# High and low parts for three chunks of the keys and for the merge's first branch, in a two-block transformer kernel

## The chip, the cores and the metric

The kernel runs on one core of a Trainium2 chip. The number compared is the device time of one execution in microseconds (us). The kernel before takes 986.09 us, the median of three runs (984.8 to 986.31). A row of the profile gives a start in us from the start of the span.

TensorE (PE in the rows) multiplies matrices into PSUM, the accumulation memory of eight banks. ScalarE (ACT), VectorE (DVE) and GpSimd (POOL) do elementwise work, and SyncE (SP) issues the transfers of the weights. Each engine works through its own queue in order; semaphores order them among each other.

## The reference, cut to what matters

256 tokens of width 1024 go through two blocks. The change lies in the first 240 us, in the first block's mixer and in the key and value projection of its cross-attention:

```python
proj = h @ w_in                                    # 1024 -> 6144
a = a_val * sigmoid(a_gate)
a = causal_dwconv(a, conv_a_w) + conv_a_b          # 31 taps, 512 channels
a = silu(layernorm(a, ln_a_g, ln_a_b)) @ w_a_out   # 512 -> 1024
p = grouped(multiscale_pool_minus_token(u_pool)) * pool_scale
c = (c_b * causal_dwconv(c_c * c_x, conv_c_w)) @ w_c_out
merged = gates[0] * a + gates[1] * p + gates[2] * c
x = x + merged @ w_o
k, v = split(mem_n @ w_xkv, 2)                     # 256 memory rows, 1024 -> 2048
```

## The kernel before, in words

**Chunks and halves.** All large weights come as one stream of chunks, each of two halves of 128 partitions by 1024 numbers (512 KB). SP loads half `c` into one of six raw buffers (`raw`, RAW = 6), as soon as half `c - 6` has left it. `C_WIN`, `C_K1`, `C_V1`, `C_POOL`, `C_MERGE`, `C_V1B`, `C_WO` are the first chunks of the input projection (24 chunks), the keys (4), three of four value chunks (3), the pool (1), the merge (4), the last value chunk (1) and the output projection (4). I write K0 to K3 for the chunks of the keys, V0 to V2 for those of the values, M0 to M3 for the merge, and "first half" and "second half" for the halves of each.

**Two ways to multiply.** A half whose number is in `NATIVE` is multiplied as it is, in float32, straight from `raw` (`project_native`), and its raw buffer comes free when TensorE has used it. Any other half is split: ScalarE rounds it to `wh` (`round_high`, L1685 in the rows), VectorE subtracts to get `wl` (`subtract`, L2183), which frees the raw buffer, and TensorE multiplies three products, high by high, high by low and low by high (`three`). There are four slots of `wh` and `wl` (SPLIT = 4), so ScalarE may round a half only when TensorE has used the split half four before it. `after(n)` lets an engine go ahead in this splitting up to two chunks behind chunk `n`; `full(n)` does so up to the next chunk and then waits until TensorE is done with chunk `n`.

**Units.** The result of a chunk (or of half a merge chunk) is a unit, and goes to one of four PSUM banks (UNITS = 4) in turn. `free_bank` makes TensorE wait until the unit four before it has been read, by ScalarE or by VectorE.

**Order around the change.** TensorE: input projection, K0 to K3 with `memn` (the normalised memory rows), V0, the sum for the layer norm's mean, V1, the sum for its variance, V2, four small pool units, then for each m of the merge the product of branch a (native, with `actT`, the output of the silu) and of branch c (split, with `cy_h` and `cy_l`), V1B, and the output projection. VectorE does the 124 instructions of the 31 taps in portions between the splits (`convolve`, L2303), then the layer norm's elementwise part, the pool's four units (L2416), and for each m the merge's products with the gates, their sum and its split for the next projection. The order on each engine is written out by hand; no scheduler changes it.

Of the kernel before, what the change touches and what calls it, by code (L numbers as in the profile page):

```python
# [28 lines left out]
ALU = mybir.AluOpType  # L29
# [7 lines left out]
P = 128  # L37
# [44 lines left out]
CHUNKS = C_FFN + 3 * FSTEPS  # L82
HALVES = 2 * CHUNKS

NATIVE = frozenset((*range(4), *range(2 * C_K1, 2 * C_K1 + 8), 2 * C_POOL, 2 * C_POOL + 1, *range(2 * C_MERGE, 2 * (C_MERGE + 4), 2),
                    *range(2 * C_K2, 2 * C_K2 + 2), *range(2 * C_FILL, 2 * C_FILL + 8), 2 * C_V2B, 2 * C_V2B + 1,
                    *range(2 * C_FFN, 2 * C_FFN + 4)))

# [117 lines left out]
def build(nc, stream, xt_in, memt_in, mem2t_in, small_in, const_in, mask_in, router_in, moe_in, gain_in, out_rows):  # L206
    ctx = ExitStack()
    with ctx:
        def sb(name, shape, dt=F32):
            return ctx.enter_context(nc.sbuf_tensor(name, shape, dt))  # L210

        def sem(name):
            return ctx.enter_context(nc.semaphore(name))
# [7 lines left out]
        xT = sb("xT", [P, DK, T])  # L221
        sq_at = -(-nc.sbuf_base // 32) * 32
        sq = sb("sq", [P, DK, T])
        memn = sb("memn", [P, 2, DK, T])
        kT = sb("kT", [P, DK, T])
        vm = sb("vm", [P, TT, D])
# [33 lines left out]
        def at(name, start, shape, dt):  # L260
            return nc.alloc_sbuf_tensor_at(name, shape, dt, offset=area_at + 4 * start)
# [55 lines left out]
        cpad_at = r.at  # L317
        cpad = r(4, T + C_K - 1)
        cy_h, cy_l = (at(n, start, [P, 4, T], F32R) for n, start in (("cy_h", cpad_at), ("cy_l", cx_at)))
        upad = r(4, T + PADW)  # L320
        ubuf = r(4, T + PADW)

# [2 lines left out]
                                 for i in range(4))  # L325
        asq = agate
        actT = memn[:, 0, 0:4, :]

        xg32 = kT
        vm_flat = vm.rearrange("p t d -> p (t d)")  # L330
# [162 lines left out]
        ln_std = sem("ln_std")  # L493
        ln_normed = sem("ln_normed")
        a_act = sem("a_act")
        pool_full = sem("pool_full")
        merged_ready = sem("merged_ready")
        scores_done = sem("scores_done")
# [213 lines left out]
        def _(pe):  # L712
            units = UnitCount()

            def matmul(out, w, x, start, stop, **kw):
                return nc.tensor.matmul(out, w, x, start=start, stop=stop, **kw)  # L716

            def wait_raw(c):

                pe.wait_ge(landed[c % RAW], 16 * (c // RAW + 1))  # L720

            def wait_split(c):
                pe.wait_ge(low_ready, split_count(c))

            def free_bank(u):

                if u >= UNITS:
                    before = u - UNITS
                    pe.wait_ge(act_free if before in ACT_UNITS else unit_free, act_count(before) if before in ACT_UNITS else freed(before + 1))

            def three(out, a_h, a_l, b_h, b_l, start, stop, **kw):

                matmul(out, a_h, b_h, start, False, **kw)
                matmul(out, a_h, b_l, False, False, **kw)
                return matmul(out, a_l, b_h, False, stop, **kw)
# [276 lines left out]
            def project_native(n, x, tile_ready=None, between=None):  # L1012

                u = units.take()
                free_bank(u)
                for j in range(2):
                    c = 2 * n + j
                    if c:
                        wait_raw(c)
                    else:  # L1020
                        pe.wait_ge(s_first, 16)
                    for k in range(DK):
                        if c == 0 and k == DK // 2:
                            wait_raw(c)
                        if tile_ready and j == 0:
                            pe.wait_ge(tile_ready, k + 1)
                        last = matmul(psum[:, u % UNITS, j * T:(j + 1) * T], raw[:, c % RAW, k * P:(k + 1) * P],
                                      x[:, k, :], k == 0, k == DK - 1)
                    last.then_inc(half_done, 1)
                    if between and j == 0:  # L1030
                        between()
# [28 lines left out]
            for n in range(C_WIN + 16, C_WIN + 24):  # L1060
                project(n, xg)
            pe.wait_ge(memn_ready, 1)
            for m in range(4):
                project_native(C_K1 + m, memn[:, 0])
                if m == 2:
                    stats(2)

            pe.wait_ge(mem_split, 1)
            project_rows(C_V1, xg)
            pe.wait_ge(ln_added, 1)  # L1070
            for c in range(2):
# [12 lines left out]
            for m in range(4):  # L1084
# [6 lines left out]
                        last.then_inc(half_done, 1)  # L1091
                if m < 3:
                    last.then_inc(pool_full, 1)
            pe.wait_ge(a_act, 4)
            pe.wait_ge(c_split, 1)
            for m in range(4):
                c = 2 * (C_MERGE + m)
                wait_raw(c)
                u = units.take()
                free_bank(u)  # L1100
                for j in range(2):
                    for k in range(4):
                        last = matmul(psum[:, u % UNITS, j * T:(j + 1) * T],
                                      raw[:, c % RAW, k * 256 + j * P:k * 256 + (j + 1) * P], actT[:, k, :],
                                      k == 0, k == 3)
                last.then_inc(half_done, 1)
                wait_split(c + 1)
                u = units.take()
                free_bank(u)
                for j in range(2):  # L1110
                    for k in range(4):
                        w = slice(k * 256 + j * P, k * 256 + (j + 1) * P)
                        last = three(psum[:, u % UNITS, j * T:(j + 1) * T], wh[:, SLOT[c + 1], w], wl[:, SLOT[c + 1], w],
                                     cy_h[:, k, :], cy_l[:, k, :], k == 0, k == 3)
                last.then_inc(half_done, 1)
            project_rows(C_V1B, xg)
            pe.wait_ge(merged_ready, 4)
            for m in range(4):
# [491 lines left out]
        def _(act):  # L1610
# [145 lines left out]
            from_unit(C_V1 + 1, 29, vm[:, :, 256:512])  # L1756
            act.wait_ge(ln_var, 1)
            fn(lnstd, psum[:, 5, 0:T], ACT.Sqrt, scale=1.0 / 512, bias=eps[:]).then_inc(ln_std, 1)
            act.wait_ge(ln_normed, 2)
            for c in range(4):  # L1760
                fn(actT[:, c, :], aacc[:, c, :], ACT.Silu, scale=sm("ln_g", c), bias=sm("ln_b", c)).then_inc(a_act, 1)
            from_unit(C_V1 + 2, 30, vm[:, :, 512:768])

            def divide(hh):

# [404 lines left out]
        def _(dve):  # L2170
# [167 lines left out]
            def short_conv(j):  # L2338
# [7 lines left out]
                                                      ALU.mult, ALU.add)  # L2346
                link(last)

            for n in range(4, 24):
                if n in (8, 9):  # L2350
                    full(C_WIN + n)
                    h = slice(2 * (n - 8), 2 * (n - 8) + 2)
                    dve.wait_ge(act_free, act_count(7))
                    tt(cpad[:, h, C_K - 1:], unit_view(n), cx[:, h, :], ALU.mult).then_inc(unit_free, 1)
                after(C_WIN + n)
                convolve(5 if n < 6 else 4)
                if n == 6:
                    window_sums()
                if n == 7:
                    window_means()  # L2360
                if n == 10:
                    dve.wait_ge(unit_free, freed(10))
                if 10 <= n < 13:
                    short_conv(n - 10)
                if n == 13:
                    dve.wait_ge(act_free, act_count(11))
                    tt(cy[:], cy[:], cb[:], ALU.mult).then_inc(c_ready, 1)
                if n == 17:
                    recip(1)
                if n == 20:  # L2370
                    normalise_memory(0, "mem_g")
# [10 lines left out]
            split_memory(0, xh, xl)  # L2382
            for n in range(4):
                after(C_K1 + n)
                convolve(10 if n < 3 else 4 * CONV_K - done[0])
            dve.wait_ge(conv_a, 4 * CONV_K)
            tt(asq[:, 0:2, :], aacc[:, 0:2, :], aacc[:, 2:4, :], ALU.add).then_inc(ln_added, 1)
            recip(2)
# [15 lines left out]
            for m in range(2):  # L2404
                h = slice(2 * m, 2 * m + 2)
                tt(aacc[:, h, :], aacc[:, h, :], two(lnrstd), ALU.mult).then_inc(ln_normed, 1)
            after(C_V1 + 2)
            dve.wait_ge(act_free, act_count(23))
            for m in range(4):
                if m < 3:  # L2410
# [8 lines left out]
                last.then_inc(unit_free, 1)  # L2419
            for m in range(4):  # L2420
                full(C_MERGE + m)
                ua, uc = units.take(), units.take()
                q = slice(2 * m, 2 * m + 2)
                tt(mt1[:], unit_view(ua), gates[:, 2 * m:2 * m + 2, :], ALU.mult).then_inc(unit_free, 1)
                tt(mt2[:], unit_view(uc), gates[:, 16 + 2 * m:18 + 2 * m, :], ALU.mult).then_inc(unit_free, 1)
                dve.wait_ge(unit_free, freed(uc + 1))
                link(tt(mt1[:], mt1[:], mt2[:], ALU.add))
                link(tt(merged[:, q, :], mt1[:], merged[:, q, :], ALU.add))
                link(v.tensor_copy(yh[:, q, :], merged[:, q, :]))
                tt(yl[:, q, :], merged[:, q, :], f32(yh[:, q, :]), ALU.subtract).then_inc(merged_ready, 1)  # L2430
                after(C_MERGE + m)
# [689 lines left out]
def _stream(a):  # L3121
# [14 lines left out]
    units(C_WIN, a["w_in"][0], WIN_ORDER)  # L3136
    s[C_POOL, 1] = a["w_pool_grp"][0].transpose(1, 0, 2).reshape(P, 1024)
    for m in range(4):
        s[C_MERGE + m, 0] = _tiles(a["w_a_out"][0], 4, 256 * m, 256)
        s[C_MERGE + m, 1] = _tiles(a["w_c_out"][0], 4, 256 * m, 256)  # L3140
    units(C_K1, a["w_xkv"][0], range(4))
    units(C_V1, a["w_xkv"][0], range(3), D, row_halves)
    units(C_V1B, a["w_xkv"][0], (3,), D, row_halves)
# [106 lines left out]
```

## Time and profile before

| | us |
|---|---|
| median of three runs | 986.09 |
| the profiled execution's own time | 987.19 |
| its span, from the first to the last instruction | 985.3 |
| PE busy with matmuls | 964.8 (98%) |
| DVE busy | 750.9 (76%) |
| ACT busy | 518.7 (53%) |
| POOL busy | 40.5 (4%) |

All figures but the first are of one profiled execution, which took 1.1 us more than the median of the runs; 1.9 us of its time lie outside the span. A PE row's duration is the time of one matmul from its issue to its end; several are on their way at a time, so the pace is read from the starts, or from the number of matmuls in a stretch. A native float32 product shows as two records.

### The profile page before, as it was taken

The page shows a single profiled execution, that of the slowest core. Times are in us where ns is not written, and L with a number is a line of the kernel's source. Part 1 is how long each engine was busy: PE and PEld are TensorE (multiplying, and loading weights), DVE is VectorE, ACT ScalarE, POOL GpSimd, SP SyncE. Part 2 cuts the span into 40 slices and gives each one's busy share as a digit, 9 for nine tenths or more (in the row PEclk, how much of TensorE's full clock was granted, in tenths as well). Part 3 has the DMA queues.
Part 4 walks back from the last instruction along what each step waited for, and adds up shares of the span by engine and source line. Part 5 has one row for each costly group of instructions (what it writes and reads, how often), then busy time and mean ns, then how long its engine had stood idle before and what let it go on. Part 6 is the DMA issues. An engine that isn't in the chain of part 4 may idle for free.

```text
span 985.3 us, 16653 instructions
## 1 busy us (share of the span) xinstructions
PE 964.8 (98%) x6545; PEld 886.5 (90%) x6545; DVE 750.9 (76%) x1137; ACT 518.7 (53%) x752; POOL 40.5 (4%) x42
## 2 busy tenths in 40 slices
PE   7999999999999999999999999999999999999997
PEld 6999998999999888888889999877999998999996
DVE  5699878779766886888868877965486289787876
ACT  4545533524453676777754635545465465555544
POOL 0002001000101000000001000000100120000000
PEclk9999999999999999999999999999999999999999
DMA  7945653456540677878873534221543255555541
GB/s 273 354 161 177 211 166 128 171 172 218 171 143 1 235 259 274 322 264 292 319 255 122 174 95 168 65 66 65 192 170 131 86 191 192 192 179 200 178 168 43
DMA packets 49601, 178.39 MB, mean 181 GB/s; under 512 B 5632, under 2 KB 5888, under 8 KB 49280
## 3 DMA queue, kind: packets, MB, share of 16 engines
q1 hardware_dynamic: 47952, 172.51, 51.3%
q10 hardware_dynamic: 1584, 4.99, 1.4%
q8 instruction: 44, 0.72, 0.3%
q14 instruction: 21, 0.17, 0.1%
HBM read 176.43 MB, written 1.05 MB: 180 GB/s over the span
## 4 chain that ended last, share of the span: by engine, by line
PE 91%; DVE 6%; issue 1%; DMA 1%; ACT 1%; DVEq 0%; SPq 0%; ACTq 0%
PE psum L716 89%; DVE wl L2183 2%; DVE work L2183 1%; DMA raw<-stream_in 1%; DVE xl L2221 1%; PE psum L958 1%; PE psum L1270 0%; DVE work L3012 0%; DVE xh L2216 0%; DVE rstd L2211 0%; DVE xT L2183 0%; ACT wh L1685 0%; DVE work L3075 0%; DVE ypair L2183 0%; ACT work L1612 0%
## 5 line engine op out<-in xcount | busy, mean ns | idle before, releaser
L1685 ACT CAST wh<-raw 128x1024 fp32r<-128x1024 f32 x292 | 303.8, 1051 | 288.4 <-PE psum L716 248.5
L2183 DVE TENSOR_TENSOR wl<-raw,wh 128x1024 fp32r<-128x1024 f32 x292 | 349.3, 1228 | 72.4 <-ACT wh L1685 69.5
L716 PE MATMUL psum<-xh,wh 128*128 128x256 f32 x976 | 275.9, 283 | 2.9 <-DVE wl L2183 2.3
L716 PE MATMUL psum<-xl,wh 128*128 128x256 f32 x976 | 273.1, 280 | 0.0
L716 PE MATMUL psum<-xh,wl 128*128 128x256 f32 x976 | 273.1, 280 | 0.0
L716 PEld LDWEIGHTS psum<-xh,wh 128*128 128x128 f32 x976 | 184.2, 189 | 6.3 <-DVE wl L2183 2.6
L716 PEld LDWEIGHTS psum<-xl,wh 128*128 128x128 f32 x976 | 184.2, 189 | 0.5
L716 PEld LDWEIGHTS psum<-xh,wl 128*128 128x128 f32 x976 | 184.2, 189 | 0.0
L716 PE MATMUL psum<-wh,slots 128*128 128x512 f32 x320 | 101.6, 390 | 0.0
L716 PE MATMUL psum<-memn,raw 128*128 128x256 f32 x320 | 73.0, 381 | 0.0
L716 PE MATMUL psum<-yh,wh 128*128 128x256 f32 x256 | 72.1, 282 | 0.2 <-DVE wl L2183 0.2
L716 PE MATMUL psum<-yh,wl 128*128 128x256 f32 x256 | 71.6, 280 | 0.0
L716 PE MATMUL psum<-yl,wh 128*128 128x256 f32 x256 | 71.4, 279 | 0.0
L716 PEld LDWEIGHTS psum<-wh,slots 128*128 128x128 f32 x320 | 60.1, 188 | 12.4
L716 PEld LDWEIGHTS psum<-memn,raw 128*128 128x128 f32 x320 | 59.4, 190 | 8.1 <-issue 0.7
L716 PE MATMUL psum<-wl,slots 128*128 128x512 f32 x160 | 62.3, 389 | 0.0
L2183 DVE TENSOR_TENSOR work<-psum,rstd 128x512 f32<-128x512 f32 x38 | 26.0, 690 | 41.1 <-PE psum L716 40.9
L2303 DVE SCALAR_TENSOR_TENSOR ypair<-work,small,ypair 128x256 f32<-128x256 f32 x120 | 54.8, 523 | 0.0
L2138 POOL TENSOR_TENSOR sq<-sq 128x512 f32<-128x512 f32 x18 | 27.0, 1501 | 551.2 <-ACT sq L1612 550.9
L716 PEld LDWEIGHTS psum<-yh,wh 128*128 128x128 f32 x256 | 48.1, 188 | 1.1 <-issue 0.7
L716 PEld LDWEIGHTS psum<-yl,wh 128*128 128x128 f32 x256 | 48.1, 188 | 0.0
L716 PEld LDWEIGHTS psum<-yh,wl 128*128 128x128 f32 x256 | 48.1, 188 | 0.0
(277 smaller groups left out, 1478.8 us busy)
## 6 DMA issues: line engine op xcount, KB each, us to landing
raw<-stream_in SPq DMA_DIRECT2D x325, 512.0 KB, 4.5
memn<-mem_t_in ACTq DMA_DIRECT2D x2, 1024.0 KB, 9.1
out_rows<-work SPq DMA_DIRECT2D x4, 256.0 KB, 2.2
const<-const_in ACTq DMA_DIRECT2D x1, 581.0 KB, 4.7
xT<-x_t_in SPq DMA_DIRECT2D x2, 256.0 KB, 4.6
xT<-x_t_in ACTq DMA_DIRECT2D x2, 256.0 KB, 5.4
raw<-stream_in SPq DMA_DIRECT2D x2, 256.0 KB, 5.3
mask<-mask_in ACTq DMA_DIRECT2D x1, 512.0 KB, 13.6
```

The costliest lines, as they stand in the source:

```text
L716: return nc.tensor.matmul(out, w, x, start=start, stop=stop, **kw)
L958: last = nc.tensor.transpose(psum[:, u % UNITS, m * T + t * P:m * T + (t + 1) * P], probs[:, (base + h) % 4, t, m * P:(m + 1) * P], ident)
L1685: nc.scalar.copy(wh[:, SLOT[c], :], raw[:, c % RAW, :]).then_inc(hi_ready, 1)
L2138: nc.gpsimd.tensor_tensor(sq[:, 0:2, :], sq[:, 0:2, :], sq[:, 2 * m:2 * m + 2, :], ALU.add).then_inc(sq_added, 1)
L2183: return v.tensor_tensor(out, a, b, op)
L2221: last = v.scalar_tensor_tensor(xl[:, k, :], xT[:, k, :], sm(name, k), f32(xh[:, k, :]), ALU.mult, ALU.subtract)
L2303: ins = v.scalar_tensor_tensor(aacc[:, c, :], x, sm("conv_w", 4 * j + c), aacc[:, c, :], ALU.mult, ALU.add)
```

## The change

1. K1 to K3 leave `NATIVE` and are split; K0 stays native. TensorE waits for the split of the memory rows (`mem_split`) after K0 and not after K3.
2. The merge: branch a is split as well. Its activations get a high part `ay_h`, made by ScalarE, and a low part `ay_l`, made by VectorE. For each m branch c now comes first and branch a second, and the waits stand ahead of the first use of each.
3. ScalarE copies the values' third unit, with the splits that stand ahead of this copy, before the norm's activation, and not after it.
4. The 124 taps are spread anew over the chunks: 96 (before: 82) by the end of the input projection, then 5, 8, 8, 7 (before: 10, 10, 10, 12).

```diff
-NATIVE = frozenset((*range(4), *range(2 * C_K1, 2 * C_K1 + 8), 2 * C_POOL, 2 * C_POOL + 1, *range(2 * C_MERGE, 2 * (C_MERGE + 4), 2),
+NATIVE = frozenset((*range(4), 2 * C_K1, 2 * C_K1 + 1, 2 * C_POOL, 2 * C_POOL + 1,
...
             pe.wait_ge(memn_ready, 1)
-            for m in range(4):
-                project_native(C_K1 + m, memn[:, 0])
+            project_native(C_K1, memn[:, 0])
+            pe.wait_ge(mem_split, 1)
+            for m in range(1, 4):
+                project(C_K1 + m, xg)
                 if m == 2:
                     stats(2)
-            pe.wait_ge(mem_split, 1)
...
-            pe.wait_ge(a_act, 4)
-            pe.wait_ge(c_split, 1)
             for m in range(4):
...
+                for i, (high, low, ready) in enumerate(((cy_h, cy_l, c_split), (ay_h, ay_l, a_split))):
+                    c = 2 * (C_MERGE + m) + i
+                    wait_split(c)
+                    pe.wait_ge(ready, 1)
+                    u = units.take()
+                    free_bank(u)
+                    for j in range(2):
+                        for k in range(4):
+                            w = slice(k * 256 + j * P, k * 256 + (j + 1) * P)
+                            last = three(psum[:, u % UNITS, j * T:(j + 1) * T], wh[:, SLOT[c], w], wl[:, SLOT[c], w],
+                                         high[:, k, :], low[:, k, :], k == 0, k == 3)
+                    last.then_inc(half_done, 1)
...
             fn(lnstd, psum[:, 5, 0:T], ACT.Sqrt, scale=1.0 / 512, bias=eps[:]).then_inc(ln_std, 1)
+            from_unit(C_V1 + 2, 30, vm[:, :, 512:768])
             act.wait_ge(ln_normed, 2)
             for c in range(4):
                 fn(actT[:, c, :], aacc[:, c, :], ACT.Silu, scale=sm("ln_g", c), bias=sm("ln_b", c)).then_inc(a_act, 1)
-            from_unit(C_V1 + 2, 30, vm[:, :, 512:768])
+            act.wait_ge(a_act, 4)
+            nc.scalar.copy(ay_h[:], actT).then_inc(a_high, 1)
...
+            TAPS = {4: 5, 5: 5, 13: 4, 14: 6, 15: 6, 16: 6, 17: 4, 18: 6, 19: 6, 20: 3, 21: 5, 22: 6, 23: 6}
...
-                convolve(5 if n < 6 else 4)
+                convolve(TAPS.get(n, 4))
...
-                convolve(10 if n < 3 else 4 * CONV_K - done[0])
+                convolve((5, 8, 8)[n] if n < 3 else 4 * CONV_K - done[0])
...
             after(C_V1 + 2)
+            dve.wait_ge(a_high, 1)
+            tt(ay_l[:], actT, f32(ay_h[:]), ALU.subtract).then_inc(a_split, 1)
             dve.wait_ge(act_free, act_count(23))
...
-                ua, uc = units.take(), units.take()
+                uc, ua = units.take(), units.take()
                 q = slice(2 * m, 2 * m + 2)
+                tt(mt2[:], unit_view(uc), gates[:, 16 + 2 * m:18 + 2 * m, :], ALU.mult).then_inc(unit_free, 1)
                 tt(mt1[:], unit_view(ua), gates[:, 2 * m:2 * m + 2, :], ALU.mult).then_inc(unit_free, 1)
-                tt(mt2[:], unit_view(uc), gates[:, 16 + 2 * m:18 + 2 * m, :], ALU.mult).then_inc(unit_free, 1)
-                dve.wait_ge(unit_free, freed(uc + 1))
+                dve.wait_ge(unit_free, freed(ua + 1))
```

The two halves of each merge chunk change places in the stream, so that the weights of branch c come first.

ScalarE around the layer norm's activation, before (`work<-psum,eps` is the square root of the variance, `memn<-ypair,small` the silu, `vm<-psum` the copy of V2's unit, the casts split weights):

```order
L1612 ACTIVATE work<-psum,eps 128x256 [waits ln_var]
L1612 ACT_TABLE_LOAD
L1612 ACTIVATE memn<-ypair,small 128x256 [waits ln_normed]
L1612 ACTIVATE memn<-ypair,small 128x256 x3
L1685 CAST wh<-raw 128x1024 [waits half_done,landed5]
L1612 ACTIVATE vm<-psum 128x2x256 [waits half_done]
L1685 CAST wh<-raw 128x1024 [waits half_done,landed1]
```

The same place on ScalarE after the change:

```order
L1611 ACTIVATE work<-psum,eps 128x256 [waits ln_var]
L1684 CAST wh<-raw 128x1024 [waits half_done,landed4]
L1684 CAST wh<-raw 128x1024 [waits half_done,landed5]
L1611 ACTIVATE vm<-psum 128x2x256 [waits half_done]
L1611 ACT_TABLE_LOAD
L1611 ACTIVATE memn<-ypair,small 128x256 [waits ln_normed]
L1611 ACTIVATE memn<-ypair,small 128x256 x3
L1763 CAST ay_h_68<-memn 128x1024 [waits a_act]
```

The copy that waits for TensorE's V2 now stands ahead of the table load, of the silu and of the new cast.

VectorE from the end of the norm to the first merge unit, before (`work<-psum,small,work` reads a pool unit, two instructions each; `memn<-psum,work` is a merge product with its gate):

```order
L2183 TENSOR_TENSOR wl<-raw,wh 128x1024 [waits hi_ready]
L2416 SCALAR_TENSOR_TENSOR work<-psum,small,work 128x256 [waits pool_full,act_free]
L2416 SCALAR_TENSOR_TENSOR work<-psum,small,work 128x256
...
L2183 TENSOR_TENSOR wl<-raw,wh 128x1024 [waits hi_ready]
L2183 TENSOR_TENSOR memn<-psum,work 128x512 [waits half_done]
```

And after:

```order
L2184 TENSOR_TENSOR wl<-raw,wh 128x1024 [waits hi_ready] x2
L2184 TENSOR_TENSOR ay_l<-memn,ay_h 128x1024 [waits a_high]
L2420 SCALAR_TENSOR_TENSOR work<-psum,small,work 128x256 [waits pool_full,act_free]
L2420 SCALAR_TENSOR_TENSOR work<-psum,small,work 128x256
...
L2184 TENSOR_TENSOR wl<-raw,wh 128x1024 [waits hi_ready] x2
L2184 TENSOR_TENSOR memn<-psum,work 128x512 [waits half_done]
```

The reading of the pool's units now stands behind the subtraction that waits for ScalarE's `ay_h`, and where one half was split two are split.

## Rows read from the trace of the kernel before

**Rows 1.** The page, busy time of each engine

```profile
PE 964.8 (98%) x6545; PEld 886.5 (90%) x6545; DVE 750.9 (76%) x1137; ACT 518.7 (53%) x752; POOL 40.5 (4%) x42
```

**Rows 2.** Waits of PE over the span: total us, times, longest

```profile
PE psum L716 <- DMA raw<-stream_in: 5.8, 1, 5.8
PE psum L716 <- DVE wl L2183: 2.5, 4, 1.3
```

**Rows 3.** Windows: length, busy us of each engine, then granted clock, DMA share, GB/s

```profile
100.00:145.00 45.00, 45.00 (x386) 44.95 (x386) 39.33 (x65) 21.75 (x25) 0.00 (x0) 1.00 0.61 195
147.96:175.83 27.87, 27.87 (x132) 24.54 (x131) 23.84 (x41) 10.62 (x16) 4.75 (x4) 1.00 0.41 132
189.10:194.80 5.70, 5.70 (x50) 5.69 (x49) 3.04 (x3) 3.62 (x6) 0.00 (x0) 1.00 0.00 0
198.24:223.40 25.16, 25.16 (x161) 23.50 (x161) 19.03 (x29) 5.24 (x5) 0.00 (x0) 1.00 0.55 186
```

**Rows 4.** Timeline of ScalarE: start, length, instruction, count

```profile
178.51 1.04 ACT L1751 CAST cy_h<-work 128x1024 fp32r<-128x1024 f32 x1
...
189.31 0.47 ACT L1612 ACTIVATE work<-psum,eps 128x256 f32<-128x256 f32 x1 [0.27 <-PE psum L716]
189.80 1.28 ACT L1612 ACT_TABLE_LOAD   x1
192.93 2.08 ACT L1612 ACTIVATE memn<-ypair,small 128x256 f32<-128x256 f32 x4 [1.85 <-DVE ypair L2183]
...
195.85 0.59 ACT L1612 ACTIVATE vm<-psum 128x512 f32<-128x512 f32 x1
```

**Rows 5.** Timeline of VectorE, keys to pool

```profile
151.72 11.51 DVE L2303 SCALAR_TENSOR_TENSOR ypair<-work,small,ypair 128x256 f32<-128x256 f32 x20
...
174.65 4.83 DVE L2303 SCALAR_TENSOR_TENSOR ypair<-work,small,ypair 128x256 f32<-128x256 f32 x12
179.51 0.69 DVE L2183 TENSOR_TENSOR ypair<-ypair 128x512 f32<-128x512 f32 x1
...
197.13 3.22 DVE L2416 SCALAR_TENSOR_TENSOR work<-psum,small,work 128x256 f32<-128x256 f32 x8
```

**Rows 6.** Timeline of VectorE, merge and output projection

```profile
204.74 1.29 DVE L2183 TENSOR_TENSOR memn<-psum,work 128x512 f32<-128x512 f32 x2 [3.26 <-PE psum L716]
...
208.59 1.22 DVE L2183 TENSOR_TENSOR wl<-raw,wh 128x1024 fp32r<-128x1024 f32 x1
211.03 1.29 DVE L2183 TENSOR_TENSOR memn<-psum,work 128x512 f32<-128x512 f32 x2 [1.23 <-PE psum L716]
...
223.62 1.29 DVE L2183 TENSOR_TENSOR memn<-psum,work 128x512 f32<-128x512 f32 x2
...
227.46 2.35 DVE L2183 TENSOR_TENSOR wl<-raw,wh 128x1024 fp32r<-128x1024 f32 x2
...
233.25 2.35 DVE L2183 TENSOR_TENSOR wl<-raw,wh 128x1024 fp32r<-128x1024 f32 x2
...
237.70 2.35 DVE L2183 TENSOR_TENSOR wl<-raw,wh 128x1024 fp32r<-128x1024 f32 x2
240.50 0.69 DVE L2183 TENSOR_TENSOR xT<-psum,xT 128x512 f32<-128x512 f32 x1 [0.45 <-PE psum L716]
```

**Rows 7.** Timeline of GpSimd, keys

```profile
152.02 4.12 POOL L2138 TENSOR_TENSOR sq<-sq 128x512 f32<-128x512 f32 x3 [63.42 <-ACT sq L1612]
156.22 0.79 POOL L2142 TENSOR_TENSOR sq<-sq 128x256 f32<-128x256 f32 x1
```

**Rows 8.** Timeline of PE around 570 us

```profile
568.17 2.37 PE L716 MATMUL psum<-cden,const 10*64 10x256 f32 x20
...
572.20 0.41 PE L716 MATMUL psum<-xh,wl 128*128 128x256 f32 x1
572.41 0.41 PE L716 MATMUL psum<-xh,wh 128*128 128x256 f32 x1
```

**Rows 9.** Window on the same place, columns as in the third group

```profile
571.00:575.00 4.00, 4.00 (x23) 4.00 (x23) 3.12 (x8) 0.00 (x0) 0.00 (x0) 0.57 0.83 250
```

More of the change, by code:

```diff
@@ L223, in build @@
         sq = sb("sq", [P, DK, T])
+        memn_at = -(-nc.sbuf_base // 32) * 32
         memn = sb("memn", [P, 2, DK, T])
@@ L319, in build @@
         cy_h, cy_l = (at(n, start, [P, 4, T], F32R) for n, start in (("cy_h", cpad_at), ("cy_l", cx_at)))
+        ah_at = 24 * T + 8
+        assert ah_at + 4 * T <= 24 * T + 4 * (T + CONV_K - 1)
+        ay_h = at("ay_h", ah_at, [P, 4, T], F32R)
         upad = r(4, T + PADW)
@@ L327, in build @@
         actT = memn[:, 0, 0:4, :]
+        ay_l = nc.alloc_sbuf_tensor_at("ay_l", [P, 4, T], F32R, offset=memn_at)
         xg32 = kT
@@ L495, in build @@
         a_act = sem("a_act")
+        a_high = sem("a_high")
+        a_split = sem("a_split")
         pool_full = sem("pool_full")
@@ L1093, in _ @@
                     last.then_inc(pool_full, 1)
-            pe.wait_ge(a_act, 4)
-            pe.wait_ge(c_split, 1)
             for m in range(4):
[L1097 to L1115, printed above, removed]
+                for i, (high, low, ready) in enumerate(((cy_h, cy_l, c_split), (ay_h, ay_l, a_split))):
[10 more added lines that the diff above has]
+                    last.then_inc(half_done, 1)
             project_rows(C_V1B, xg)
@@ L3138, in _stream @@
     for m in range(4):
-        s[C_MERGE + m, 0] = _tiles(a["w_a_out"][0], 4, 256 * m, 256)
-        s[C_MERGE + m, 1] = _tiles(a["w_c_out"][0], 4, 256 * m, 256)
+        s[C_MERGE + m, 0] = _tiles(a["w_c_out"][0], 4, 256 * m, 256)
+        s[C_MERGE + m, 1] = _tiles(a["w_a_out"][0], 4, 256 * m, 256)
     units(C_K1, a["w_xkv"][0], range(4))
```

## The prediction

> **What bounds the kernel now.** I read first the page's busy times: PE is at work for 964.8 of the span's 985.3 us, VectorE for 76% [rows 1]. Then the waits of PE: 5.8 us for the first transfer and 2.5 us for splits in the whole span [rows 2]. So a microsecond less of matmul work shortens the kernel by as much, if the other engines keep up. Then windows, for the pace of each way to multiply. Three products: 386 matmuls in 45.00 us, 0.1166 each, so a half of 24 takes 2.80 us. Native: K0 to K3 are 64 products in 27.87 us, less 0.43 for one sum's product, so a half of eight takes 3.43 us [rows 3]. The merge, four native and four split units, takes 25.16 us, so a split unit there is 2.85 and a native one 3.44. Last the timelines of ScalarE and VectorE from 150 to 240 us, for who comes late once PE is faster.
>
> **Part 1, keys.** Six halves save 0.63 each: PE comes to V0 3.8 us sooner, at 172.0 and not 175.83. Does VectorE follow? It gains six subtractions, 1.15 us each where they stand in pairs [rows 6], and loses 14 of 42 taps, 0.40 each (12 in 4.83) [rows 5], to the input projection. There VectorE is busy for 39.33 of 45 us [rows 3], and its 14 taps are 5.6 us over that stretch of waits, which I cost at nothing; the price if that cover is gone is 0.40 a tap. ScalarE gains six casts of 1.04 and is busy for 10.62 of these 27.87 us [rows 3, 4]; they hide in its waits for PE. SP's loads wait for the last use of a raw buffer; that was PE's end of a native half and is now VectorE's subtraction, which comes sooner for all but K0, so I cost the transfers at nothing (0.39 to 0.61 of the transfer engines' time there is used [rows 3], and a late one would cost its delay in full). The last links before the norm's mean: the second half of V1 can be rounded only when PE ends K3 (172.0), one cast (1.04, the shape of the 178.51 row) [rows 4] makes that 173.2, its subtraction 174.35, seven taps 177.1, the sum of 0.69 [rows 5] 177.8. PE has V0 done at 172.0 + 5.7 = 177.7 [rows 3]. So 0.1 us of stall, and about half a microsecond of slack in the taps ahead of it. From there PE goes through two sums of 0.86 and V1 and V2 of 5.70 each: it ends V2 at about 190.95, where before it was 194.8 [rows 3]: 3.85 us ahead.
>
> **Part 2, ScalarE's copy ahead of the activation.** This is where I see the gain go. Before, the square root ran at 189.31, the table load right behind it at 189.80 while nothing else was due, the silu at 192.93, and the copy at 195.85 [rows 4]. Now the copy waits for V2 (190.95, seen at 191.15), and what stands behind it in the queue comes after it, although the norm is ready at about 189.1. Step by step: copy to 191.65 (the next instruction may follow 0.50 later), load 1.28, silu 2.08, so 195.05; `ay_h`, a cast of the same size as `cy_h`, 1.04, so 196.15; `ay_l` on VectorE, 1.22 with 1.15 to the next instruction, so 197.35 [rows 4, 6]. Behind it on VectorE wait the eight instructions that read the pool's units, 3.22 us for eight [rows 5], which took no input from the norm. The first bank comes free after two, at 198.2. PE is done with the pool at 190.95 + 3.44 = 194.4, and its first merge product needs that bank. Before, the reading began at 197.13 [rows 5] and PE started the merge at 198.24 [rows 3]. Now it starts at 198.3. All 3.85 us of part 1 have turned into an idle PE of 3.9 us.
>
> **Part 3, merge.** Eight split units of 2.85 are 22.8 us where 25.16 were: 2.4 less for PE. But VectorE has 3.85 us of merge work for each m (204.74 to 208.59) and now two subtractions, 2.27, not one: 6.1 us against PE's 5.7. Before it had 1.23 us of idle time per m [rows 6]. It begins m = 0 at 198.3 + 5.7 + 0.2 = 204.2 (before 204.74) and m = 3 at 204.2 + 3 x 6.12 = 222.55 (before 223.62): 1.1 us sooner. PE waits some tenths for splits of M3 and V1B.
>
> **Part 4, output projection.** From m = 3 on VectorE is without a gap to 240.05 and then waits 0.45 us for PE's second chunk of the output projection [rows 6]. After the change PE itself waits for the first split of that chunk, 10.85 us behind the start of m = 3, and ends it 5.6 us later: 222.55 + 10.85 + 5.6 + 0.25 = 239.25, against 240.50. So 1.2 us are left, and behind this place the order and the work are the same on every engine.
>
> **The sum without the clock.** 3.85 + 2.4 less matmul time, 5.0 of it lost to waits: -1.2 us. Bounds: -0.3 if part 1 or the queue of ScalarE is a microsecond later, -2.4 if the table load doesn't delay the silu.
>
> **The clock.** PE has no gap near 3.9 us in the kernel before. The nearest case is at 568.17: 2.37 us with nothing but products of ten rows [rows 8], and then the granted clock is 0.57 over the next 4.00 us, where 1.0 is 2.4 GHz and 0.5 the lower level of 1.2 GHz [rows 9]; matmuls start every 0.21 us there and not every 0.117 (572.20 and 572.41) [rows 8]. Price: 4.00 x 0.43 = 1.7 us of full-speed work. After a real gap of 3.9 us I expect the same. Part of the low stretch may fall into the gap, so I bound the price by 0 (no fall) and 1.7 and take 1.2, nearer to the row. It falls on M0, whose end starts VectorE's chain, so it counts in full. The sum: 987.19 - 1.2 + 1.2 = 987.2 for the profiled execution, which was 1.1 above the median of the runs: 986.1.
>
> The Trainium skill has a rule that speaks against this change ("TensorE: Matmul & The Clock Gate", HAM oscillation): work that comes in bursts with idle stretches between them is multiplied at half speed at the start of each burst, since the gate is opened by activity alone. The row at 568 us agrees that thin work is enough; by the rule the clock term stands, without it the kernel would be 1.2 us faster.
>
> **Rivals.**
> *The clock stays high.* For it: waits of PE of 1.3 us at most elsewhere [rows 2] don't tell; the 2.37 us at 568 speak against it. Then -1.2: 984.9.
> *PE's saving arrives.* If the reading of the pool's units isn't behind the norm in effect, or PE bound all: -3.85 - 2.4 = -6.3, at least the -2.4 of the merge with some of part 1; I put it at -4 as a middle, 982.1. Against it: the new order of VectorE, and 6.1 against 5.7 us per m.
> *Slower: VectorE late in the keys.* GpSimd folds squares from 152.02 to 157.0 [rows 7], and 20 taps took 11.51 us there [rows 5] and not 7.9: 3.6 us lost to 4.9 of GpSimd's work. I counted that VectorE idles until 154 for casts and then loses 2.4 us on two subtractions and 5 taps. Part 1 has 0.5 us of slack. If the loss is the full 4.9, the mean's sum is late by 4.9 - 2.4 - 0.5 = 2.0 us; V2, the copy, the silu and the merge all are. With the clock's price: 988.1. It decides from 0.5 us of loss beyond mine. Against it: the taps of that place have gone, and the subtractions have 3 us until PE needs them.
> The Trainium skill says ("SBUF — State Buffer", Who interferes with whom) that an instruction of VectorE with two inputs in SBUF and one of GpSimd exclude each other, the later one blocking fully. By it, all overlap would be lost time, by my estimate 3.0 us in place of 2.4; the row, 3.6 of 4.9, lies between that and none.
>
> **Chances.** Clock falls, net zero: 0.45. Clock stays: 0.22. Saving arrives, wholly or in part: 0.12. VectorE late: 0.16. Anything else, as a transfer that comes late: 0.05. A difference of under 0.2% (2 us) can't be told from none here. Faster by more: the third and an eighth of the first two, 0.20. Slower by more: most of the fourth and some of the first, 0.20. Same: 0.60. The range, 984.0 to 988.3, leaves out the full saving and the worst of the late VectorE.
>
> **What would show it.** V0 starts near 172.1, V2 ends near 191. ScalarE's table load stands at 191.7 and the silu ends near 195. PE idles from 194.4 to 198.3. The granted clock is below 1 in a window from there to 204. VectorE has no idle time between the m of the merge, and m = 3 starts between 222.5 and 224. The first chunk of residuals after PE's wait comes near 239.3 to 240.7. I am wrong if V0 starts later than 173, if PE doesn't idle ahead of the merge, or if the clock stays at 1.00 with a time above 986.

## The result, and the profile after

The changed kernel takes 987.55 us, the median of 22 runs (984.5 to 988.88), against 986.08 for the kernel before, of 22 runs too. The ratio is 1.0014, with a 95% interval from 1.0008 to 1.002: 1.4 us slower, small but clear of the noise of so many runs. The profiled execution took 987.6 us, its span is 985.8. The ratio of an experiment is to executions of the kernel before on the same chip (medians 985.7 us for experiments 1 to 4, 985.68 for 5 to 7, 985.1 for 8 and 9), and leaves out one of them that took 1204.04 us.

The page of the changed kernel, and PE's waits over the span (total us, times, longest):

```profile
PE 960.9 (97%) x6625; PEld 885.4 (90%) x6625; DVE 761.3 (77%) x1148; ACT 529.4 (54%) x763; POOL 42.1 (4%) x42
```

```profile
PE psum L723 <- DVE work L2420: 3.8, 1, 3.8
PE psum L723 <- issue: 3.2, 3, 1.4
PE psum L723 <- DVE wl L2184: 3.0, 6, 1.3
...
PE psum L723 <- DVE ypair L2184: 0.3, 1, 0.3
```

PE is busy for 3.9 us less than in [rows 1], and has two waits that the kernel before doesn't have: 3.8 us for `work` of L2420, the reading of the pool's units, and 0.3 us for the sum of the norm's mean. (The line numbers of the changed file are shifted: L723 is the matmul of L716, L2184 and L2420 are VectorE's L2183 and L2416. Each experiment shifts them by a few more.)

ScalarE's timeline after, which answers to [rows 4]:

```profile
186.16 0.47 ACT L1611 ACTIVATE work<-psum,eps 128x256 f32<-128x256 f32 x1 [0.27 <-PE psum L723]
186.53 1.99 ACT L1684 CAST wh<-raw 128x1024 fp32r<-128x1024 f32 x2
191.84 0.60 ACT L1611 ACTIVATE vm<-psum 128x512 f32<-128x512 f32 x1 [3.32 <-PE psum L723]
192.45 1.28 ACT L1611 ACT_TABLE_LOAD   x1
193.75 2.07 ACT L1611 ACTIVATE memn<-ypair,small 128x256 f32<-128x256 f32 x4
195.85 1.04 ACT L1763 CAST ay_h<-memn 128x1024 fp32r<-128x1024 f32 x1
```

The copy waits 3.32 us for V2. The table load, the silu and `ay_h` follow it without a gap. VectorE's timeline after, which answers to [rows 5] and [rows 6]:

```profile
188.45 1.29 DVE L2184 TENSOR_TENSOR ypair<-ypair,work 128x512 f32<-128x512 f32 x2
189.66 2.35 DVE L2184 TENSOR_TENSOR wl<-raw,wh 128x1024 fp32r<-128x1024 f32 x2
196.93 1.23 DVE L2184 TENSOR_TENSOR ay_l<-memn,ay_h 128x1024 fp32r<-128x1024 f32 x1 [4.91 <-ACT ay_h L1763]
198.07 3.22 DVE L2420 SCALAR_TENSOR_TENSOR work<-psum,small,work 128x256 f32<-128x256 f32 x8
201.21 2.35 DVE L2184 TENSOR_TENSOR wl<-raw,wh 128x1024 fp32r<-128x1024 f32 x2
206.56 1.29 DVE L2184 TENSOR_TENSOR memn<-psum,work 128x512 f32<-128x512 f32 x2 [3.00 <-PE psum L723]
...
212.68 1.28 DVE L2184 TENSOR_TENSOR memn<-psum,work 128x512 f32<-128x512 f32 x2
...
218.79 1.28 DVE L2184 TENSOR_TENSOR memn<-psum,work 128x512 f32<-128x512 f32 x2
...
224.90 1.28 DVE L2184 TENSOR_TENSOR memn<-psum,work 128x512 f32<-128x512 f32 x2
...
241.79 0.69 DVE L2184 TENSOR_TENSOR xT<-psum,xT 128x512 f32<-128x512 f32 x1 [0.45 <-PE psum L723]
```

VectorE has the norm ready by 189.7, makes two splits until 192.0, and then idles for 4.91 us in front of the low part of branch a, with the reading of the pool's units behind it. From m = 0 on it goes through the merge without a wait, 6.11 us per m. The row at 241.79 is the one at 240.50 in [rows 6]: 1.29 us later. PE's first products of the merge, then windows on the gap and behind it (length, busy us of PE, PEld, DVE, ACT, POOL, then granted clock, DMA share, GB/s):

```profile
199.09 0.36 PE L723 MATMUL psum<-cy_h,wh 128*128 128x256 f32 x1 [3.84 <-DVE work L2420]
...
199.90 0.41 PE L723 MATMUL psum<-cy_h,wl 128*128 128x256 f32 x1
200.11 0.41 PE L723 MATMUL psum<-cy_h,wh 128*128 128x256 f32 x1
```

```profile
195.30:199.00 3.70, 0.00 (x0) 0.00 (x0) 2.07 (x4) 3.46 (x5) 0.00 (x0) 1.00 0.81 280
199.00:203.00 4.00, 3.91 (x20) 3.94 (x21) 4.00 (x8) 0.00 (x0) 0.00 (x0) 0.57 0.68 271
```

PE has done nothing for 3.7 us; in the next 4.00 us, 0.57 of the 2.4 GHz is granted, as in [rows 9], and 20 matmuls start where 34 would. The merge's first product starts at 199.09, the first of m = 1 at 206.36, and VectorE begins with m = 0 at 206.56: PE takes 7.3 us for the work of 5.7.

### The profile page after: what moved, and what is told of

It reads as the page before. It is cut to its first block, busy times and chain, and to the rows that moved or that the text cites. A ratio compares the mean times of both kernels' runs of the same rounds, so it can differ in the third digit from the quotient of the medians.

```text
span 985.8 us, 16844 instructions
## 1 busy us (share of the span) xinstructions
PE 960.9 (97%) x6625; PEld 885.4 (90%) x6625; DVE 761.3 (77%) x1148; ACT 529.4 (54%) x763; POOL 42.1 (4%) x42
## 4 chain that ended last, share of the span: by engine, by line
PE 87%; DVE 9%; ACT 1%; issue 1%; DMA 1%; DVEq 0%; SPq 0%; ACTq 0%
PE psum L723 86%; DVE wl L2184 3%; DVE work L2184 1%; DMA raw<-stream_in 1%; DVE xl L2222 1%; DVE memn L2184 1%; PE psum L965 1%; PE psum L1269 0%; DVE work L3016 0%; ACT wh L1684 0%; DVE xh L2217 0%; DVE rstd L2212 0%; DVE xT L2184 0%; DVE ypair L2304 0%; DVE ypair L2184 0%
## 5 line engine op out<-in xcount | busy, mean ns | idle before, releaser
L1684 ACT CAST wh<-raw 128x1024 fp32r<-128x1024 f32 x302 | 313.8, 1051 | 289.7 <-PE psum L723 270.4
L2184 DVE TENSOR_TENSOR wl<-raw,wh 128x1024 fp32r<-128x1024 f32 x302 | 362.3, 1233 | 65.0 <-ACT wh L1684 62.1
L723 PE MATMUL psum<-xh,wh 128*128 128x256 f32 x1024 | 289.7, 283 | 2.7 <-DVE wl L2184 2.3
L723 PE MATMUL psum<-xl,wh 128*128 128x256 f32 x1024 | 286.6, 280 | 0.0
L723 PE MATMUL psum<-xh,wl 128*128 128x256 f32 x1024 | 286.4, 280 | 0.0
L723 PEld LDWEIGHTS psum<-xh,wh 128*128 128x128 f32 x1024 | 193.2, 189 | 6.1 <-DVE wl L2184 2.6
L723 PEld LDWEIGHTS psum<-xl,wh 128*128 128x128 f32 x1024 | 193.2, 189 | 0.6
L723 PEld LDWEIGHTS psum<-xh,wl 128*128 128x128 f32 x1024 | 193.2, 189 | 0.0
L723 PE MATMUL psum<-wh,slots 128*128 128x512 f32 x320 | 101.7, 391 | 0.0
L723 PE MATMUL psum<-yh,wh 128*128 128x256 f32 x256 | 72.0, 281 | 0.5 <-DVE wl L2184 0.5
L723 PE MATMUL psum<-yh,wl 128*128 128x256 f32 x256 | 71.5, 279 | 0.0
L723 PE MATMUL psum<-yl,wh 128*128 128x256 f32 x256 | 71.4, 279 | 0.0
L723 PEld LDWEIGHTS psum<-wh,slots 128*128 128x128 f32 x320 | 60.1, 188 | 12.5
L723 PE MATMUL psum<-wl,slots 128*128 128x512 f32 x160 | 62.3, 389 | 0.0
L2184 DVE TENSOR_TENSOR work<-psum,rstd 128x512 f32<-128x512 f32 x38 | 26.0, 690 | 41.3 <-PE psum L723 41.1
L723 PEld LDWEIGHTS psum<-yh,wh 128*128 128x128 f32 x256 | 48.1, 188 | 1.7 <-issue 1.2
L723 PEld LDWEIGHTS psum<-yl,wh 128*128 128x128 f32 x256 | 48.1, 188 | 0.0
L723 PEld LDWEIGHTS psum<-yh,wl 128*128 128x128 f32 x256 | 48.1, 188 | 0.0
L723 PE MATMUL psum<-memn,raw 128*128 128x256 f32 x160 | 37.6, 383 | 0.0
L3016 DVE SCALAR_TENSOR_TENSOR work<-work,small 128x256 f32<-128x256 f32 x88 | 36.7, 479 | 0.7 <-ACT work L1611 0.7
```

The source lines that it names most:

```text
L1684: nc.scalar.copy(wh[:, SLOT[c], :], raw[:, c % RAW, :]).then_inc(hi_ready, 1)
L2184: return v.tensor_tensor(out, a, b, op)
L3016: v.scalar_tensor_tensor(fconv[:, f % 2, j, :], upad2[:, f % 2, j, tap:tap + T], w, fconv[:, f % 2, j, :], ALU.mult, ALU.add).then_inc(fco ...
```

## The experiments

**1. ScalarE's copy behind the silu.** Everything else is the changed kernel.

```diff
-            from_unit(C_V1 + 2, 30, vm[:, :, 512:768])
+            after(C_V1 + 2)
             act.wait_ge(ln_normed, 2)
...
             nc.scalar.copy(ay_h[:], actT).then_inc(a_high, 1)
+            from_unit(C_V1 + 2, 30, vm[:, :, 512:768])
```

> The changed kernel with one edit on ScalarE: the copy of the values' third unit stands behind the silu and the high part of branch a again (the splits that stood ahead of it stay). Theory (the copy holds back the silu and all behind it): the table load runs right behind the square root, at about 186.7 to 190, the silu starts when the norm is ready (189.8) and not at 193.75, the high part is made by 193 and the low part by 194.3, the first pool bank comes free at 195.1, PE idles 0.3 us at most ahead of the merge, and the granted clock stays 1.00. The merge's first unit starts at 195.3 and not at 199.1, and ends its m = 0 in 5.7 us and not in 7.3: 3.8 + 1.6 = 5.4 us less, 982.1 us. Rival 1 (VectorE's 6.1 us per m would set the end anyway): the gap goes, the time falls by less than 1 us. Rival 2 (the pool's units wait for something else, as the transfers): nothing moves.

Measured: 980.53 us; the ratio to the kernel before is 0.9949 (0.9936 to 0.9962), 5.0 us faster than it, and faster than both kernels. ScalarE and VectorE in it:

```profile
188.45 1.28 ACT L1611 ACT_TABLE_LOAD   x1
189.75 2.08 ACT L1611 ACTIVATE memn<-ypair,small 128x256 f32<-128x256 f32 x4
191.86 1.04 ACT L1763 CAST ay_h<-memn 128x1024 fp32r<-128x1024 f32 x1
192.81 0.59 ACT L1611 ACTIVATE vm<-psum 128x512 f32<-128x512 f32 x1
```

```profile
192.94 1.23 DVE L2185 TENSOR_TENSOR ay_l<-memn,ay_h 128x1024 fp32r<-128x1024 f32 x1 [1.00 <-ACT ay_h L1763]
194.08 3.22 DVE L2421 SCALAR_TENSOR_TENSOR work<-psum,small,work 128x256 f32<-128x256 f32 x8
...
201.04 1.29 DVE L2185 TENSOR_TENSOR memn<-psum,work 128x512 f32<-128x512 f32 x2 [1.48 <-PE psum L723]
```

The silu starts at 189.75 and not at 193.75, though V2 ends as late as in the changed kernel (PE starts the pool at 191.55, there at 191.64), and m = 0 reaches VectorE at 201.04 and not at 206.56: 5.5 us, where 5.4 were expected. The rival that VectorE would set the end anyway falls. The median is 1.6 us lower than expected; the last section has a likely source.

**2. VectorE reads the pool's units ahead of the low part.** ScalarE is left as changed.

```diff
-            dve.wait_ge(a_high, 1)
-            tt(ay_l[:], actT, f32(ay_h[:]), ALU.subtract).then_inc(a_split, 1)
             dve.wait_ge(act_free, act_count(23))
...
                 last.then_inc(unit_free, 1)
+            dve.wait_ge(a_high, 1)
+            tt(ay_l[:], actT, f32(ay_h[:]), ALU.subtract).then_inc(a_split, 1)
```

> The changed kernel with one edit on VectorE: the eight instructions that read the pool's four units stand ahead of the low part of branch a, not behind it; ScalarE is left as it is, so the silu is as late as in the changed kernel. Theory (PE waits for a bank, not for the activation): the banks are free by 196, branch c's first unit, which needs nothing of branch a, starts at 195.3 and takes 2.85 us, and the low part is ready at 198.1, just as PE wants it. Idle time of PE 0.3 us at most, clock 1.00, 5.3 us less than the changed kernel: 982.2 us. If the activation itself bounds (rival), PE waits after branch c's first unit for the low part and the gain is 2 us or less.

Measured: 982.25 us, ratio 0.9962 (0.9949 to 0.9975). VectorE in it:

```profile
192.73 3.39 DVE L2418 SCALAR_TENSOR_TENSOR work<-psum,small,work 128x256 f32<-128x256 f32 x8 [0.76 <-PE psum L723]
196.88 1.23 DVE L2184 TENSOR_TENSOR ay_l<-memn,ay_h 128x1024 fp32r<-128x1024 f32 x1 [0.77 <-ACT ay_h L1763]
201.31 1.29 DVE L2184 TENSOR_TENSOR memn<-psum,work 128x512 f32<-128x512 f32 x2 [0.93 <-PE psum L723]
```

The low part comes no sooner than in the changed kernel (196.88 and 196.93), and m = 0 is still at 201.31. So PE waited for a bank and not for the activation. With branch c first, the activation of branch a may come as late as the end of branch c's unit, 2.85 us behind the first product, at no cost; here PE starts branch a at 198.21, half a microsecond behind the last product of branch c.

**3. Filler in the gap.** PE does useless work into an unused bank; everything else is the changed kernel.

```diff
+            for _ in range(16):
+                matmul(psum[:, 4, 0:P], ones, ones, True, True)
```

> The changed kernel with 16 extra native products of ones by ones, 128x128, into an unused PSUM bank, between the pool and the merge on PE. By the pace of native 128-column products in the trace before (four records in 0.44 us) they take 3.5 of the 3.8 us in which PE would idle, and delay nothing. Theory (the clock fell after the gap, and cost 1.6 us): the granted clock stays 1.00 over 199 to 203, m = 0 of the merge takes 5.7 us and not 7.3, and the time is 1.5 us less than the changed kernel: 986.0, that of the kernel before. Rival (the slow first units have another cause, as the start of the split weights or transfers at 99% of their engines at that time): m = 0 stays at 7.3 us, no change of time.

Measured: 984.08 us, ratio 0.9987 (0.9978 to 0.9996), where the changed kernel has 1.0014. PE's timeline, then a window, in it:

```profile
194.49 3.73 PE L723 MATMUL psum<-ones 128*128 128x128 f32 x32
198.49 0.36 PE L723 MATMUL psum<-cy_h,wh 128*128 128x256 f32 x1 [0.27 <-DVE work L2422]
```

```profile
199.00:203.00 4.00, 4.00 (x36) 4.00 (x35) 3.96 (x7) 1.05 (x1) 0.00 (x0) 1.00 0.56 214
```

The merge waits as long for its bank, but the clock stays at 1.00, and from the first product (198.49) to VectorE's m = 0 (204.43 in its timeline) it is 5.9 us and not 7.5: the clock's price is 1.5 us. The transfers are not the cause of the slow first unit: from 199.5 to 200.5 the transfer engines are fully used in both kernels (DMA share 1.03 here, 1.00 in the changed kernel), and PE starts 11 matmuls here, at clock 1.00, and 7 there, at 0.53. 16 products that compute nothing make the kernel faster. Its whole gain over the changed kernel is 2.7 us by the ratios, more than the 1.5 expected.

**4. The keys and the taps alone**, on the kernel before.

```diff
-NATIVE = frozenset((*range(4), *range(2 * C_K1, 2 * C_K1 + 8), ...
+NATIVE = frozenset((*range(4), 2 * C_K1, 2 * C_K1 + 1, ...
...
-                convolve(5 if n < 6 else 4)
+                convolve(TAPS.get(n, 4))
...
```

> The kernel before with the first and the fourth part of the change alone: three chunks of the keys split, taps spread anew; the merge, its order and ScalarE's copy as before. Theory (the keys' 3.8 us are real and were lost only at the pool): V2 ends at 191.6, the silu runs at 189.8 to 191.9, the pool is read in 194.2 to 197.3, PE starts the merge at 195.1 without a gap, and the whole is 3.2 to 3.8 us less than before: 982.6. Rival (VectorE or the transfers give the gain back later, in the output projection): less than 1.5 us.

Measured: 982.05 us, ratio 0.9968 (0.9956 to 0.998). On VectorE:

```profile
193.62 3.22 DVE L2418 SCALAR_TENSOR_TENSOR work<-psum,small,work 128x256 f32<-128x256 f32 x8
201.23 1.29 DVE L2184 TENSOR_TENSOR memn<-psum,work 128x512 f32<-128x512 f32 x2 [3.26 <-PE psum L716]
```

Against 197.13 and 204.74 in [rows 5] and [rows 6] both are 3.5 us sooner, and it reaches the end: 3.6 us by the medians, 3.2 by the ratio (2.0 to 4.3).

**5. The merge and the copy alone.** The changed kernel with the keys and taps of before.

```diff
-NATIVE = frozenset((*range(4), 2 * C_K1, 2 * C_K1 + 1, ...
+NATIVE = frozenset((*range(4), *range(2 * C_K1, 2 * C_K1 + 8), ...
...
```

> The changed kernel with the keys and the taps of the kernel before: K0 to K3 native, taps 5, 5, 4, ..., 10, 10, 10, 12. So this is the merge's change alone, with ScalarE's copy ahead of the silu. Theory (the gap hangs on the end of V2 by a fixed chain and is there without the keys): V2 ends at 194.8, the silu at 198.9, the low part at 201.2, the first pool bank is free at 202.1, PE idles 3.9 us from 198.2, the clock falls, m = 0 takes 7.3 us, VectorE starts m = 3 at 228.0 where the kernel before starts it at 223.6: 4.4 us slower than before, 990.2. The changed kernel, at 987.5 in its many runs, is then this one less 2.7 to 3.8 us for the keys. Rival (the gap is the keys' saving waiting for something fixed in time, as a transfer or the memory's second norm): PE starts the merge at 199 here too, and the time is that of the kernel before less 1, 985.

Measured: 990.38 us, ratio 1.0047 (1.0032 to 1.0061). PE's wait there:

```profile
201.49 0.55 PE L723 MATMUL psum<-cy_h,wh 128*128 128x256 f32 x1 [3.83 <-DVE work L2419]
```

The gap is 3.83 us, as in the changed kernel (3.84), and has moved with the end of V2: PE ends V2 at 194.04 and starts the merge at 201.49, both 2.40 us later than in the changed kernel. The granted clock is 0.57 over 201 to 205. The parts add up within the noise: by the medians -3.6 of the keys and +4.7 of the merge give +1.1, by the ratios -3.2 and +4.6 give +1.4, and +1.4 is measured.

**6. The taps of before** in the changed kernel.

```diff
-                convolve(TAPS.get(n, 4))
+                convolve(5 if n < 6 else 4)
...
-                convolve((5, 8, 8)[n] if n < 3 else 4 * CONV_K - done[0])
+                convolve(10 if n < 3 else 4 * CONV_K - done[0])
```

> The changed kernel with the taps of the kernel before (14 more of them behind the input projection: portions 10, 10, 10, 12). Theory (VectorE has about half a microsecond of slack between the keys and the norm's mean, and what comes late there is late at the end): 14 taps of 0.40 are 5.6 us, less the waits they fill; the mean's sum is made at 182.6 and not at 178.4, PE idles 4.2 us ahead of it, the end of V2 and all behind it move by 4.2 us, up to 5.8 if the clock falls after that gap too. 992 us, 991.5 to 993.5. Rival (the stretch has more room than that, since the taps fill waits for casts): 988 to 989.

Measured: 993.52 us, ratio 1.0078 (1.0063 to 1.0092).

```profile
182.47 2.07 PE L723 MATMUL psum<-ypair,ones 128*128 128x256 f32 x4 [4.74 <-DVE ypair L2184]
...
205.48 0.55 PE L723 MATMUL psum<-cy_h,wh 128*128 128x256 f32 x1 [3.83 <-DVE work L2420]
```

PE waits 4.74 us for the mean's sum, and the two products behind the wait (four records) take 2.07 us and not about 1.0: the clock falls after this gap too (0.50 over 181 to 185), and again after the one ahead of the merge (0.50 over 205 to 209). So the taps' new spread is what makes the split keys a gain, worth 6 us here, and two gaps cost two falls. Each of these falls costs more than the one of the changed kernel: the clock is low from the first product behind the gap, and for longer. From 205.48 to the first product of m = 1 at 213.92 it is 8.4 us for the work of 5.7, so 2.7 us are lost where the changed kernel loses 1.6 behind an equal gap. The profiled execution, 995.99 us, is the slowest of the five, with a mean granted clock of 0.989; three of the others have 0.993 and took 993.0 to 993.5 us.

**7. Both edits of 1 and 2.**

> Both edits of the first two experiments: ScalarE's copy behind the silu, and VectorE reads the pool's units ahead of the low part. Theory (each alone took the whole gap away, and VectorE's 6.1 us per m of the merge set the rest): the merge starts at 195.2 as with either alone, VectorE's m = 3 starts between 219.3 and 219.7, and the time is that of the first experiment: 980.5, or 1.6 more where the clock falls near 570 us. Rival (the two gains add in part): up to 1 us less.

Measured: 980.42 us, ratio 0.9944 (0.9931 to 0.9958), the same as experiment 1. VectorE starts m = 3 at 219.08, where experiment 1 has 219.38. Once PE has no gap, the second way round it buys nothing.

**8. The merge's high part on ScalarE**, on top of experiment 1, with experiment 1 again on the same chip (**9**).

```diff
-            high.upto(2 * (C_MERGE + 3) + 1)
+            high.upto(2 * C_MERGE + 3)
+            for m in range(4):
+                high.upto(2 * (C_MERGE + m) + 5)
+                act.wait_ge(m_sum, m + 1)
+                nc.scalar.copy(yh[:, 2 * m:2 * m + 2, :], merged[:, 2 * m:2 * m + 2, :]).then_inc(m_high, 1)
...
-                link(tt(merged[:, q, :], mt1[:], merged[:, q, :], ALU.add))
-                link(v.tensor_copy(yh[:, q, :], merged[:, q, :]))
+                tt(merged[:, q, :], mt1[:], merged[:, q, :], ALU.add).then_inc(m_sum, 1)
+                rest.upto(2 * (C_MERGE + m) + (5 if m < 3 else 4))
+                dve.wait_ge(m_high, m + 1)
                 tt(yl[:, q, :], merged[:, q, :], f32(yh[:, q, :]), ALU.subtract).then_inc(merged_ready, 1)
```

> The first experiment's kernel (copy behind the silu) with one more edit in the merge: the high part of each merged pair is made by ScalarE and not by VectorE, which does the splits of the next chunk in between. Theory (with the gap gone VectorE bounds the merge at 6.1 us per m): VectorE has 0.46 us less per m, 5.66, and PE's 5.70 bounds; m = 3 starts 17.1 us after m = 0 and not 18.3, and the whole is 1.0 to 1.3 us less than the first experiment: 979.4. Rival (PE bounds the merge, or what is gained there is waited away in the output projection, where VectorE is without a gap too): less than 0.4 us, 980.3.

> The first experiment's kernel once more, on the same chip as the one before it, so that a difference of one us can be told: 980.5 us as before, if no clock fall near 570 us comes into it.

Measured: 978.6 us, ratio 0.994 (0.9927 to 0.9954), and 981.0 us, ratio 0.9963 (0.9949 to 0.9976), for experiment 1 again. VectorE in the eighth:

```profile
200.70 1.29 DVE L2191 TENSOR_TENSOR memn<-psum,work 128x512 f32<-128x512 f32 x2 [1.48 <-PE psum L725]
...
206.36 1.29 DVE L2191 TENSOR_TENSOR memn<-psum,work 128x512 f32<-128x512 f32 x2
...
217.69 1.29 DVE L2191 TENSOR_TENSOR memn<-psum,work 128x512 f32<-128x512 f32 x2
```

It is 5.66 us per m now and m = 3 comes 17.0 us behind m = 0, not 18.3: the 1.3 us expected, so VectorE did bound the merge. The medians differ by 2.4 us. The traces explain 1.3 of them; for the rest there is no row, and with five executions each it may be chance: those of the eighth fall into 978.3 to 978.6 us (three) and 980.8 to 981.0 (two), and the means differ by 1.7. This is the fastest kernel of the study, 6.5 us (by the medians) below the kernel before.

## Why the prediction was right, step by step

The time, 987.55 us, lies in the range (984.0 to 988.3), and the change is below the 0.2% that I called no difference; the number, 986.1, was 1.4 us low. The case that I gave the most chance, a gap and then a clock fall, is what the profile shows. Two signs that I named missed: m = 3 starts at 224.90 (I had up to 224), and the residuals come at 241.79 (up to 240.7). In the line on the transfers, 0.39 should read 0.41 [rows 3]; nothing hangs on it.

- *Keys.* I had 3.85 us at V2's end. ScalarE saw V2 done at 191.84 where I had 191.15. 0.23 us of it are a later start of the profiled execution (ScalarE's unit ahead of the keys is copied at 148.39, before at 148.16), 0.3 lie at the mean's sum (V1 starts at 179.22, where I had 178.66, 0.23 of it again the later start), and 0.1 in V1 and V2. The profiles of the experiments, with the taps of before or after, copy that unit anywhere from 147.4 to 148.3, so the 0.23 can't be put down to the change. The 14 taps moved into the input projection cost PE nothing, as I had it: 386 matmuls from 100 to 145 us as in [rows 3], with VectorE busy for 42.97 of the 45 us. Experiment 4 shows that the saving is real: 3.6 us by the medians. GpSimd's folding beside VectorE cost what I had counted: two subtractions took 4.08 us in the trace after and not 2.35, the five taps behind them 2.54 and not 2.07, so 2.2 us, and I had 2.4. GpSimd lost time too, which I had left out: 4.86 and 1.60 us for the work of 4.12 and 0.79 in [rows 7]. The rival of a late VectorE didn't come true; experiment 6 shows how near it was.
- *ScalarE's copy.* Right, in place and size: table load, silu, `ay_h`, `ay_l` and the first two of the eight readings end in a PE gap of 3.84 us; I had 3.9. Experiments 1 and 2 take either link out, and the gap goes. That the chain hangs on V2 and on nothing fixed in time is shown by experiment 5.
- *Merge.* 6.11 us per m, I had 6.1; m = 3 starts 18.34 us after m = 0, I had 18.35. Experiment 8 shows that this is VectorE's bound.
- *The clock.* Right in kind, too small in size: I took 1.2 us, between 0 and 1.7. It is 1.57 (7.3 us in place of 5.7) in the trace after and 1.5 by experiment 3. The term was mis-sized because I let part of the low stretch fall into the gap; it began only at 199.7, when PE worked again. My upper bound of 1.7 isn't one either: experiment 6 pays 2.7 behind an equal gap. What sets the length of the low stretch stays open.
- *The account.* My 1.2 us sooner and 1.2 later should have put the row of 240.50 at 240.45. It is at 241.79: 0.23 later start, about 0.45 for V2, 0.37 for the clock, and 0.3 that I can't place. That this equals the 1.4 us by which the number was low is luck. Of the 1.3 us by which this row is later than before, 0.9 are left at the last of the `cden` products (687.0 and 687.9) and 0.5 at the end of the span, and for the profiled execution I had 987.2, 0.4 low. The other 1.1 come from my last step: I took 1.1 off for the distance of the profiled execution from the median, and the one of the changed kernel (987.6) stands at its median.
- *The Trainium skill's rules.* The one on bursts ("TensorE: Matmul & The Clock Gate", HAM oscillation) held in kind: 3.8 us of nothing, and from 0.6 us into the merge half the clock. The same rule doesn't explain why the thin work near 570 us, which I had taken as its sign, lowers the clock in some executions only. The one on VectorE and GpSimd ("SBUF — State Buffer", Who interferes with whom) would by my estimate have cost VectorE 3.0 us; the rows give 2.2.

## What to carry to other kernels

A wait moved ahead in an in-order queue delays everything behind it, also what had been free to run in the meantime: here a copy that nobody needed early held back a table load, a silu and the cast to `ay_h`, and through them a bank. Read from each queue what stands behind the moved wait, and who needs the last of it. Where the engine that bounds comes to stand still for some microseconds, add the price of its slow start to the gap; products that compute nothing can be cheaper than standing still. And two parts of one change are worth measuring apart: here one part gives 3.6 us and the other takes 4.7, and one moved line turns the sum from +1.4 into -5.0 by the ratios (-4.3 between executions of like clock, as the next section shows).

## What the runs showed of the hardware that I had not expected

The fall of the clock near 570 us [rows 8] is in some profiled executions and not in others, with the same thin work ahead of it. The products with `cden` are a marker: from the first to the last of them is 118.8 us in the kernel before (568.2 to 687.0), 118.9 after, 118.8 in experiments 2 and 6, 118.9 in 8; it is 117.3 in experiments 1, 3, 5 and 9 and 117.4 in 4 and 7. In the first group the clock falls within 4 us behind the first of these products, in the second it stays at 1.00 there. One summary row of each kind, the kernel before and experiment 1 (name, count, durations, first and last start, shapes):

```profile
L716 PE MATMUL psum<-cden,const x28: 374/374/477, 568.2 to 687.0; 10*64 10x256 f32 x20, 4*128 4x256 f32 x8
```

```profile
L723 PE MATMUL psum<-cden,const x28: 374/374/478, 563.4 to 680.7; 10*64 10x256 f32 x20, 4*128 4x256 f32 x8
```

So such a fall costs 1.5 us. It belongs to the execution and not to the kernel, as far as the mean granted clock of each execution can tell (it doesn't say where the clock fell). Of the 16 executions of the kernel before beside experiments 1 to 4, ten have a mean of 0.996 or 0.997 and a median of 986.1 us, six have 0.998 or more and a median of 984.8, and no time of one group lies in the other. Of the changed kernel's 22, ten have 0.993 to 0.995, with a median of 987.9, and twelve have 0.996 or more, with 986.5. On the chip of experiments 5 to 7 the groups of the kernel before overlap, so something else moves the time as well.

All five executions of experiment 1 have 0.998 or more. Against the executions of the kernel before with as high a mean they are 4.3 us faster (980.5 and 984.8), which is what the traces show: m = 3 starts at 219.38 and at 223.62. The rest of its 5.0 us fits a fall near 570 that ten of those 16 executions pay and these five don't. Whether the kernel has a part in that is not shown; the same kernel, run again as experiment 9, has a mean of 0.996 in two executions of five. For experiment 3, nine of 11 have 0.998 or more, so the same is likely for its extra 1.2 us. What decides whether the clock falls there is left open.
